# A fused transformer kernel: the order of two steps in VectorE's loop over attention units

## What is computed

```python
def hybrid_mixer(h, w_in, ..., w_branch, w_gate, b_gate, w_out):
    u = h @ w_in
    y_a = short_conv_mixer(u_a, conv_a_w)
    y_n = nsa_mixer(u_nq, u_nkv, u_ng, nsa_qk_gain, cmp_pe, cmp_w1, cmp_w2)
    y_g = gated_deltanet_mixer(u_gqkv, u_gz, u_gb, u_ga, ...)
    branches = jnp.einsum('bsrc,rcd->bsrd', jnp.stack([y_a, y_n, y_g], axis=2), w_branch)
    gates = jax.nn.sigmoid((h @ w_gate + b_gate)).reshape(b, s, N_BRANCH, dm)
    merged = jnp.sum(gates * branches, axis=2)
    return merged @ w_out
```

```python
    s = jnp.where(ok, jnp.einsum(...) * scale - slopes * dist, NEG_INF)
    p = jax.nn.softmax(s, axis=-1)
    o = gate_0 * o_c + gate_1 * o_s + gate_2 * o_w
```

## Time and profile before

| | before |
|---|---|
| median of three runs | 2054.31 us |
| profiled execution, time | 2053.02 us |
| profiled execution, span | 2051.2 us |
| mean granted TensorE clock (share of full) | 0.953 |
| TensorE busy | 1845.5 us, 90% |
| VectorE busy | 1007.7 us, 49% |
| ScalarE busy | 662.1 us, 32% |
| chain that ended last, by engine | PE 76%, DVE 9%, DMA 9%, ACT 3% |

### The profile page before, as it was taken

The page is one execution under the profiler, slowest core; times in us unless marked ns, Lnnn a source line. Parts: engine busy times, 40 slices in busy tenths (PEclk is TensorE's granted clock), DMA queues, the critical chain, the costliest instruction groups (busy, mean ns, idle before and its releaser), DMA issues.

```text
span 2051.2 us, 30790 instructions
## 1 busy us (share of the span) xinstructions
PE 1845.5 (90%) x12687; PEld 1524.0 (74%) x12687; DVE 1007.7 (49%) x1404; ACT 662.1 (32%) x941; POOL 21.6 (1%) x14
## 2 busy tenths in 40 slices
PE   5999948999699988969998989988885999999998
PEld 3999938999699976769997889877773444444443
DVE  3878478886584445355545776366523111111111
ACT  3434215343344434344444623446411000000000
POOL 0000000000000000000000102000000000000000
PEclk8999979999899999989998989999997999999999
DMA  9989506997294431235441332433232999999996
GB/s 396 379 320 332 201 31 231 350 338 279 86 359 171 184 113 62 93 123 192 181 182 60 129 116 95 150 130 121 93 123 115 420 426 425 426 427 426 426 426 280
DMA packets 44583, 483.05 MB, mean 235 GB/s; under 512 B 4944, under 2 KB 5200, under 8 KB 5200
## 3 DMA queue, kind: packets, MB, share of 16 engines
q1 hardware_dynamic: 44352, 480.74, 59.6%
q10 hardware_dynamic: 144, 1.05, 0.1%
HBM read 480.72 MB, written 1.05 MB: 235 GB/s over the span
## 4 chain that ended last, share of the span: by engine, by line
PE 76%; DVE 9%; DMA 9%; ACT 3%; issue 1%; SPq 0%; DVEq 0%; ACTq 0%
PE psG L361 43%; PE psA L361 22%; PE psS L361 9%; DMA ring<-stream 9%; DVE rstd L1723 1%; DMA X<-x_in 1%; DVE mem L1762 1%; DVE parts L1970 1%; DVE H L1733 1%; DVE parts L1694 0%; ACT parts L1402 0%; DVE mem L1985 0%; ACT mem L1569 0%; DVE X L1771 0%; PE psS L1093 0%
## 5 line engine op out<-in xcount | busy, mean ns | idle before, releaser
L361 PE MATMUL psG<-parts 128*128 128x256 f32 x6016 | 783.8, 290 | 47.3 <-DVE parts L1748 34.3
L361 PEld LDWEIGHTS psG<-parts 128*128 128x128 f32 x6016 | 761.0, 198 | 57.3 <-issue 52.6
L361 PE MATMUL psA<-parts 128*128 128x256 f32 x2112 | 267.3, 283 | 0.0
L1694 DVE TENSOR_TENSOR parts<-ring,parts 128x2048 fp32r<-128x2048 f32 x88 | 201.4, 2289 | 121.8 <-ACT parts L1270 121.8
L361 PEld LDWEIGHTS psA<-parts 128*128 128x128 f32 x2112 | 259.4, 192 | 0.3 <-issue 0.3
L361 PE MATMUL psS<-ring,mem 128*64 128x512 f32 (+1 forms) x1032 | 229.4, 594 | 12.9 <-DMA ring<-stream 11.2
L1270 ACT ACTIVATE parts<-ring 128x2048 fp32r<-128x2048 f32 x88 | 168.3, 1913 | 102.6 <-PE psA L361 101.9
L361 PEld LDWEIGHTS psS<-ring,mem 128*64 128x64 f32 (+1 forms) x1032 | 72.7, 137 | 165.2 <-issue 131.2
L1685 DVE SCALAR_TENSOR_TENSOR mem<-ring,silc,mem 128x1536 f32<-128x1536 f32 (+1 forms) x98 | 138.9, 1417 | 2.7 <-issue 0.2
L1970 DVE TENSOR_TENSOR parts<-ring,parts 128x1024 fp32r<-128x1024 f32 x76 | 95.1, 1257 | 87.2 <-ACT parts L1402 86.1
L1617 ACT ACTIVATE mem<-psS 128x512 f32<-128x512 f32 x16 | 9.6, 597 | 368.1 <-PE psS L361 368.1
(11 more groups left out here) (318 smaller groups left out, 1414.7 us busy)
## 6 DMA issues: line engine op xcount, KB each, us to landing
ring<-stream SPq DMA_DIRECT2D x304, 1536.0 KB, 8.8
X<-x_in SPq DMA_DIRECT2D x1, 1024.0 KB, 17.4
mem<-masks ACTq DMA_DIRECT2D x1, 1024.0 KB, 4.9
x_out<-X SPq DMA_DIRECT2D x1, 1024.0 KB, 4.8
cst<-consts SPq DMA_DIRECT2D x1, 240.0 KB, 2.6
cols<-cols_in SPq DMA_DIRECT2D x1, 224.0 KB, 2.5
```

Source lines behind the costliest of these rows:

```text
L361: return nc.tensor.matmul(out, lhsT, rhs, start=start, stop=stop, skip_group_check=True)
L1694: V.tensor_tensor(WG[f % 2][:, 1, :], chunk(c, 0, 2 * SLOT), WG[f % 2][:, 0, :], ALU.subtract).then_inc(sem("lo_gu"), 1)
```

## The change

Only VectorE's loop over the units is edited. `tick(48+2p)` and the conditional `outcome_low` are put ahead of `scaled(p)` and `largest(p+1)`.

```diff
                 largest(0)
                 for p in range(11):
-                    scaled(p)
-                    largest(p + 1)
                     tick(48 + 2 * p)
                     if p and p % 3 == 0:
                         outcome_low(p // 3 - 1)
+                    scaled(p)
+                    largest(p + 1)
                     tick(49 + 2 * p)
                 scaled(11)
                 tick(70)
```

## The result

The change made the kernel slower: a median of 2103.99 us (2100.72 to 2105.8, four runs) against 2053.66 us for the kernel before beside it (2049.58 to 2054.85). The ratio is 1.0245, with a 95% interval of 1.0232 to 1.0257: 50.3 us. The prediction was 2105 us. The profiled execution took 2101.93 us, its span is 2099.9 us.

A forecast was written before the change was run, and what follows sets the result against it. TensorE's list was taken to set the pace in the changed stretch. Gate waits 28.9, branch iterations 7.7 and clock 14.3 us sum to 50.9 on 2053.02 us; with the median 1.3 us higher, 2105 us, range 2089 to 2118.

The forecast's parts named there:

- The wait in a gate iteration: p = 2 to 5, 8 to 10: turn(p) starts 4.2 us later, behind its fill's end; 28.9 us net in all.
- The branch iterations: p = 0, 1, 6, 7: merge waits go, but late scaled costs 1.4, 2.0, 2.3, 2.0 us; together 7.7 us lost.
- F + 3.8: p = 1: turn(1) was forecast to start 3.8 us after F, the end of fill(48+2p).
- The clock: Slow TensorE matmuls at a lower granted clock behind waits: 14.3 us, between 0 and 25.
- the eight new cold resumptions: p = 1 to 5, 8 to 10: slow matmuls behind idle times of 3.8 to 4.2 us, 2.0 us each, 16.0 together.
- The 2.8 us of cover: product's waits for copy come to be covered where the fill ahead is slower: -2.8 us in the clock term.
- The sum: 28.9 + 7.7 + 14.3 = 50.9 us on the profiled 2053.02 us; median forecast 2105 us.
- Nothing taken back later: Expert stage stays as long: held by the stream, whose six-chunk ring can run no further ahead while TensorE is late.
- The clock did fall: Answers the rival that the clock holds: waits added, TensorE resuming at full clock, 2091 us; chance 0.12.
- the highest price seen before: Rival: every cold resumption costs 2.8 us and nothing is covered, 2116 us; chance 0.10.
- the merges might decide: Rival: scaled(p) ready in time, four merge waits and two cold resumptions go, 2044 us; chance 0.03.
- the 1.89 us idle time: Ahead of the odd fill in p = 1, before the change: read as too short to lower the clock.

The follow-up runs named there:

- e4: Changed kernel, but low(51+2p) put behind largest(p+1), so scaled(p) no longer waits for the high and low parts: 2061.16 us, ratio 1.0048 to the kernel before.
- e1: Kernel before, with the new order only in the branch iterations p = 0, 1, 6, 7: 2060.96 us, ratio 1.0045.
- e5: Changed kernel plus 28 extra matmuls on TensorE ahead of the wait of turn(p), p = 1 to 10: 2083.32 us, ratio 1.0148 to the kernel before.
- e6: Kernel before, with branch iterations ordered scaled(p), merge of slot 48+2p, largest(p+1), low(51+2p) on VectorE: 2046.02 us, ratio 0.9965.
- e8: Kernel before, with the VectorE edit of e6 and the ScalarE edit of e7 together: 2042.22 us, ratio 0.9947.
- e2: Kernel before, with the new order only in the gate iterations p = 2 to 5 and 8 to 10: 2094.33 us, ratio 1.0209.
- e7: Kernel before, with ScalarE's copy(p) put ahead of soft(p+1): 2048.60 us, ratio 0.9984.
- e3: Kernel before, with only largest(p+1) moved behind tick(48+2p) and outcome_low, scaled(p) staying ahead: 2073.17 us, ratio 1.0105.
- e9: Kernel of e8 plus 36 extra matmuls ahead of turn(0) and 24 ahead of turn(11): 2037.88 us, ratio 0.9933 to the kernel before.

## Why the prediction was right, point by point

- *The wait in a gate iteration, 4.2 us, seven times, 28.9 us.* Measured 4.13 to 4.17 us each, 29.1 in all, 28.6 net of what `turn` waited before. Its parts hold: 1.56 us to the start of `low`, 2.56 for `low` and `scaled`. e4 leaves 1.5 for `scaled` alone and so 2.7 for what stood ahead of it.
- *The branch iterations, 7.7 us, none with a gain.* The waits came as worked out in p = 1 (F + 3.8), 6 (4.80 us after the fill's end) and 7 (4.09). The waits of the four iterations were 12.03 us before (7.45 ahead of the odd fills, and the 4.58 of p = 0), and the waits for `scaled` that replace them are 19.36: 7.3 more. e1 measures 10.5 us for these four iterations with their clock, where the prediction's terms give 7.7 + 2.0 + 1.1 = 10.8.
- *The clock, 14.3 us.* By the difference to e5's durations, the eight new cold resumptions cost 3.0, 2.4, 1.5, 3.0, 2.3, 2.0, 1.5 and 1.5 us (p = 1 to 5, 8 to 10): 17.2, a mean of 2.15 where 2.0 was taken. Those of p = 6 and 7 cost 2.8 and 3.0 instead of 1.4 and 1.5, 2.9 more where I had 1.1. The 2.8 us of cover came in full. Net 17.3: this term was 3 us too small.
- *The sum.* 28.6 + 7.3 + 17.3 = 53.2 for a stretch that grew by 52.9, and 50.9 had been said. To the start of `turn(11)` it took 171.0 us, where 168 had been said. That the median met the forecast within 1 us is in part luck: the clock term was 3 us too small, and the rest of the profiled execution happened to be 4 us shorter. Of these 4 us, 2.4 lie ahead of `fill(48)`, where nothing was edited; its start lies anywhere from 1351.9 to 1356.7 us in the traces here.
- *Nothing taken back later.* From `fill(71)` to the end the kernel took 571.9 us before and 570.1 after, a difference within the scatter of one kernel, and the experts 476.7 and 476.0.
- *The rivals.* The clock did fall, each time: e5 separates its part. Three of the resumptions passed the highest price seen before, 2.8 us, but the mean stayed far below it. By the rule cited from the Trainium skill ("TensorE: Matmul & The Clock Gate", HAM oscillation) every one of the eight waits would be paid, and every one was. That the merges might decide is refuted by e1. Their gain is real, but the order of the change gives it away; e6 and e8 take it (7.2 and, with the ScalarE edit, 11.0 us).

One sentence of the argument does not hold. I read from the 1.89 us idle time that so short a wait leaves the clock alone. In e2 and in e7 the same wait in the same place was followed by a slow fill, while in e7 a wait of 2.27 us was not. First the row of e2, then those of e7:

```profile
1380.27 4.60 PE L361 MATMUL psG<-parts 128*128 128x256 f32 x24 [1.89 <-issue]
```

```profile
1375.49 4.61 PE L361 MATMUL psG<-parts 128*128 128x256 f32 x24 [1.89 <-issue]
...
1435.15 3.11 PE L361 MATMUL psG<-parts 128*128 128x256 f32 x24 [2.27 <-issue]
```

The clock granted to `fill(51)` was 1.00 in the profile of before (1377.6 to 1381.0) and 0.59 in e2 (1380.3 to 1384.5). TensorE's instructions up to there are the same, but its clock had not been: `fill(49)`, behind the first unit's wait, had 0.66 of full speed before and took 4.34 us, and in e2 it had 0.50 and took 5.46, as long as in e7. Whether this is the reason was not tested. The spread is wider than these rows. A wait of 1.77 us was followed by a slow fill in e6 (first rows), and one of 3.12 us by a fill at full clock in e3 (last rows):

```profile
1424.70 0.65 PE L361 MATMUL psG<-mem 15*64 15x256 f32 x4 [1.77 <-ACT mem L1579]
1425.30 4.62 PE L361 MATMUL psG<-parts 128*128 128x256 f32 x24
```

```profile
1454.93 0.87 PE L361 MATMUL psG<-mem 128*64 128x256 f32 x8 [3.12 <-ACT mem L1579]
1455.73 3.14 PE L361 MATMUL psG<-parts 128*128 128x256 f32 x24
```

So waits between 1.8 and 3.1 us fall on either side, and one trace gives no bound for them. That a wait of 3.8 us or more was followed by slow matmuls holds for this stretch in every trace here.

## What to carry to other kernels

In a list that an engine works through in order, look at what each step waits for and who waits for it: work that another engine needs soon must not stand behind a wait for something that is needed late, and here 2.66 us of low-urgency work ahead of `scaled` made most of a loss of 50 us. A step made of parts of different urgency (merge, low part) is best split before it is moved. And price an idle time of TensorE with its resumption: behind 4.2 us of waiting came another 2 us of slow matmuls.

## What had not been expected of the hardware

Matmuls that nobody needs, put in the waits, saved 20.2 us in e5 and 3.1 to 4.3 us in e9, against the same kernels without them. And the clock's answer to a wait of about 2 us was not the same in two executions in which TensorE had the same instructions up to there (fill of 3.11 us in the profile of before, 4.60 in e2, both behind 1.89 us).
